# Splitting weight chunks in pairs instead of one by one, in a one-layer transformer kernel

## The reference

```python
x = layer_norm(a * x + 0.5 * swiglu(x, ffn1_gate, ffn1_up, ffn1_down), ...)   # d_ff 5504
x = layer_norm(a * x + hybrid_mixer(x, w_in, cmp_..., w_out), ...)            # stick-breaking and sparse attention
x = layer_norm(a * x + memory_cross_attention(x, mem, mem_wq, mem_wk, mem_wv, mem_wo), ...)
x = layer_norm(a * x + 0.5 * swiglu(x, ffn2_gate, ffn2_up, ffn2_down), ...)
```

## Time and profile before

| what | value |
| --- | --- |
| median of 3 runs | 2330.62 us (2328.92 to 2330.88) |
| profiled execution, span from first to last instruction | 2327.1 us |
| median of the runs less that span | 3.5 us |
| mean granted TensorE clock | 0.990 |
| TensorE matmul busy | 2263.6 us (97%) |
| VectorE busy | 1218.7 us (52%) |
| ScalarE busy | 1019.0 us (44%) |

### The profile page before, as it was taken

How to read it: one execution, slowest core, us unless ns; L and a number is a source line. 1 busy time by engine, 2 the same in 40 slices (tenths; PEclk the granted TensorE clock), 3 DMA queues, 4 the chain that set the end, 5 groups by cost and what they waited for, 6 DMA issues and landing times.

```text
span 2327.1 us, 26221 instructions
## 1 busy us (share of the span) xinstructions
PE 2263.6 (97%) x10486; PEld 1883.4 (81%) x10486; DVE 1218.7 (52%) x1269; ACT 1019.0 (44%) x1088; POOL 48.1 (2%) x34
## 2 busy tenths in 40 slices
PE   8999999999999999999999999997999999999996
PEld 6888888888888788888888877786888888898885
DVE  4544544455446545467556664456544454454445
ACT  4444444344334455555454443334444444443332
POOL 0000000000001100000000020001000000000001
PEclk9999999999999999999999999998999999999998
DMA  7555555465555455557346544453555555575552
GB/s 254 188 191 184 195 181 197 163 239 190 193 193 212 156 184 175 177 168 272 120 134 218 180 163 145 152 192 126 189 189 185 193 182 196 169 241 193 192 192 80
DMA packets 217084, 427.17 MB, mean 184 GB/s; under 512 B 6832, under 2 KB 23472, under 8 KB 216368
## 3 DMA queue, kind: packets, MB, share of 16 engines
q1 hardware_dynamic: 214336, 413.16, 52.5%
q10 hardware_dynamic: 2672, 12.93, 1.5%
HBM read 423.97 MB, written 2.10 MB: 183 GB/s over the span
## 4 chain that ended last, share of the span: by engine, by line
PE 93%; DVE 4%; ACT 1%; DMA 1%; issue 1%; POOL 0%; ACTq 0%; DVEq 0%; POOLq 0%
PE ps_A L489 45%; PE ps_B L489 42%; PE ps_T L505 2%; DVE wlo L921 2%; DVE x_tok L1359 1%; PE ps_T L864 1%; PE ps_T L851 1%; ACT whi L911 0%; PE ps_B L767 0%; PE ps_T L793 0%; DVE x_tok L1364 0%; DMA raw<-in_mem_wk_dram 0%; DMA stage<-in_mem_dram 0%; PE ps_T L638 0%; PE ps_T L802 0%
## 5 line engine op out<-in xcount | busy, mean ns | idle before, releaser
L921 DVE TENSOR_TENSOR wlo<-raw,whi 128x1024 fp32r<-128x1024 f32 (+1 forms) x792 | 965.9, 1222 | 1048.4 <-ACT whi L911 1047.4
L911 ACT ACTIVATE whi<-raw 128x1024 fp32r<-128x1024 f32 (+1 forms) x792 | 827.6, 1047 | 1196.9 <-PE ps_A L489 638.5
L489 PE MATMUL ps_A<-whi,xT_hi 128*128 128x512 f32 (+1 forms) x704 | 275.3, 391 | 8.4 <-DVE wlo L921 4.5
L489 PE MATMUL ps_A<-whi,xT_lo 128*128 128x512 f32 (+1 forms) x704 | 272.4, 387 | 0.0
L489 PE MATMUL ps_A<-wlo,xT_hi 128*128 128x512 f32 (+1 forms) x704 | 272.2, 387 | 0.0
L489 PE MATMUL ps_B<-whi,xT_hi 128*128 128x512 f32 (+1 forms) x704 | 270.3, 384 | 0.0
L489 PE MATMUL ps_B<-wlo,xT_hi 128*128 128x512 f32 (+1 forms) x704 | 270.3, 384 | 0.0
L489 PE MATMUL ps_B<-whi,xT_lo 128*128 128x512 f32 (+1 forms) x704 | 270.3, 384 | 0.0
L489 PEld LDWEIGHTS ps_A<-whi,xT_hi 128*128 128x128 f32 x704 | 133.3, 189 | 35.5 <-issue 8.8
L489 PEld LDWEIGHTS ps_A<-whi,xT_lo 128*128 128x128 f32 x704 | 133.1, 189 | 25.5
L489 PEld LDWEIGHTS ps_A<-wlo,xT_hi 128*128 128x128 f32 x704 | 133.4, 189 | 24.4
(11 more groups left out here) (279 smaller groups left out, 2864.2 us busy)
## 6 DMA issues: line engine op xcount, KB each, us to landing
raw<-in_ffn_gate_dram SPq DMA_DIRECT2D x80, 1024.0 KB, 4.9
raw<-in_ffn_up_dram SPq DMA_DIRECT2D x80, 1024.0 KB, 4.8
raw<-in_ffn_down_dram SPq DMA_DIRECT2D x80, 1024.0 KB, 5.1
raw<-in_w_in_dram SPq DMA_DIRECT2D x44, 1024.0 KB, 4.9
raw<-in_mem_wk_dram SPq DMA_DIRECT2D x16, 1024.0 KB, 5.1
raw<-in_mem_wv_dram SPq DMA_DIRECT2D x16, 1024.0 KB, 5.1
raw<-in_w_out_dram SPq DMA_DIRECT2D x16, 1024.0 KB, 5.1
raw<-in_mem_wq_dram SPq DMA_DIRECT2D x16, 1024.0 KB, 5.1
```

Of the source, the lines that this page charges most:

```text
L489: mm = pe.matmul(ps[pair][:, t * W:t * W + n], lhs[a][:, kt, t * P:(t + 1) * P], w[:, slot, q * n:(q + 1) * n], start=first and q == 0 and ...
L911: act.activation(whi[:, c % AHEAD, 0:n], raw[:, slot, o:o + n], ACT.Copy).then_inc(hi_made, 1)
L921: dve.tensor_tensor(wlo[:, c % AHEAD, 0:n], raw[:, slot, o:o + n], whi[:, c % AHEAD, 0:n].bitcast(F32), ALU.subtract).then_inc(lo_made, 1)
```

## The change

One ScalarE instruction and one VectorE instruction now split two neighbouring chunks, 128x2048 elements, where the chunks are full. The ring of four places is used as two places of two chunks. `make_hi` and `make_lo` do nothing for even c; for odd c they treat chunks c-1 and c together. `make_hi` waits until both chunks that held the place are multiplied, and the semaphores go up by 2. TensorE's code, the DMAs and the number of bytes in SBUF are the same.

```diff
+        def pair_of(c):
+
+            slot, s0, n, last = c // 2 % NRAW, (c - 1) % AHEAD, size(c - 1), size(c)
+            if last == n:
+                return [raw[:, slot, 0:2 * n].rearrange("p (s w) -> p s w", s=2), whi[:, s0:s0 + 2, 0:n],
+                        wlo[:, s0:s0 + 2, 0:n]]
+            return [raw[:, slot, 0:n + last]] + [w[:, s0:s0 + 2, :].rearrange("p s w -> p (s w)")[:, 0:n + last]
+                                                 for w in (whi, wlo)]
+
         def make_hi(act, c, i=None):
 
-            if c >= C_END:
+            if c >= C_END or c % 2 == 0:
                 return
-            slot, n = c // 2 % NRAW, size(c)
-            o = c % 2 * (CHUNK if n == CHUNK // 2 else n)
-            if c % 2 == 0:
-                act.wait_ge(landed[slot], plus(i, 32, 16 * (c // 8 + 1)))
+            w, hi, lo = pair_of(c)
+            act.wait_ge(landed[c // 2 % NRAW], plus(i, 32, 16 * (c // 8 + 1)))
             if c >= AHEAD:
                 act.wait_ge(multiplied, plus(i, 16, c - AHEAD + 1))
-            act.activation(whi[:, c % AHEAD, 0:n], raw[:, slot, o:o + n], ACT.Copy).then_inc(
-                hi_made, 1)
+            act.activation(hi, w, ACT.Copy).then_inc(hi_made, 2)
 
         def make_lo(dve, c, i=None):
 
-            if c >= C_END:
+            if c >= C_END or c % 2 == 0:
                 return
-            slot, n = c // 2 % NRAW, size(c)
-            o = c % 2 * (CHUNK if n == CHUNK // 2 else n)
+            w, hi, lo = pair_of(c)
             dve.wait_ge(hi_made, plus(i, 16, c + 1))
-            dve.tensor_tensor(wlo[:, c % AHEAD, 0:n], raw[:, slot, o:o + n],
-                              whi[:, c % AHEAD, 0:n].bitcast(F32), ALU.subtract).then_inc(
-                lo_made, 1)
+            dve.tensor_tensor(lo, w, hi.bitcast(F32), ALU.subtract).then_inc(lo_made, 2)
```

## The result

The changed kernel takes 2352.16 us (median of 4 runs, 2349.84 to 2354.4), the kernel before 2329.77 us on the same chips: ratio 1.0098, 95% interval 1.0083 to 1.0112. That is 22.4 us slower; forecast was 15.6 us, 2346.2 us, with a range of 2337 to 2360. Every run on record lies 1.7 to 1.9 us above its own span, so the profiled execution of the kernel before (2328.92 us) was one of the two faster of its four runs (2328.7, 2328.92, 2330.62 and 2330.88 us); of the 3.5 us that the forecast added to the span, 1.8 belong to that execution and 1.7 are the scatter of the runs. The mean granted clock of the changed kernel's profile is 0.985 (0.990 before).

The account below looks back on a forecast made before the run. TensorE, busy 97% of the span, was taken as the bound, with its waits for splits deciding. Terms 3.8 + 3.6 + 1.2 + 0.3 + 6.2 + 0.5 = 15.6 us on 2327.1, plus 3.5 for the runs: 2346.2 us, range 2337 to 2360.

Parts of the forecast that it names:

- the clock falls in CMP: Rival, 8%: TensorE idles 1.2 us in each 3.3 in CMP and drops to 1.2 GHz; +7 us, 2353.
- Saved engine time is worth nothing: Over some 396 pairs ScalarE gets 80 us back and VectorE 60, all inside idle time: 0 on the path.
- Plain blocks keep 0.86 us of slack: In plain blocks a pair's latency of 4.58 us stays under TensorE's 5.44 us of cover, costing 0.
- The rival that these blocks stall: Rival, 8%: latency over 5.44 us makes each of about 350 plain pairs pay the excess; about 2400 us.
- Matmul spacing by instruction traffic: Rival, 5%, faster: splits' instruction traffic spaces the matmuls, so halving their number shortens each chunk; 2314 at 0.04 us a chunk.
- Start, 3.6: At the kernel's start chunk 0 waits for chunk 1 too, and chunk 2's low part ends later again; 3.6 us.
- Short pairs, 3.8: Stalls of 0.42 us before each of two down products and 0.50 at six down-block ends; 3.8 us.
- Norms 1 and 2, 0.6 each: First two norms: later first chunk of w_in, less a slow-clock chunk hidden in K0; net 0.6 us each.
- The schedule's +2.9: At a norm, first chunk of w_in comes at 32.1 us from the down product's end instead of 29.2.
- Third norm, 0.3: One split between the third norm's pieces grows from 1.21 to 2.30 us, mostly taken back; 0.3 us (0 to 1.1).
- CMP, 6.2: In CMP the two-place loop takes 6.5 us, a pair every 3.3, and the second pair enters late; +6.2 us.
- Rest, 0.5: w_in, FILL and memory attention: only about 0.5 us (0 to 2), in V2 and at the first wq block's end.

Follow-up runs that it names:

- e3: Changed kernel with single chunks at the start, the down blocks' beginnings and in CMP, pairs elsewhere: 2330.34 us, ratio 1.0005 to the kernel before.
- e7: Changed kernel with the pair's ScalarE copy in the plain blocks of FFN 1 cut into 4 instructions of 512 elements: 2348.02 us, one run.
- e8: Changed kernel with the pair's ScalarE copy in the plain blocks of FFN 1 cut into 16 instructions of 128 elements: 2375.54 us, one run.
- e2: Changed kernel with single chunks at the start (chunks 0 to 3) and for the first two chunks of each down block: 2339.62 us, ratio 1.0039.
- e6: Changed kernel with ScalarE still copying pairs, but VectorE subtracting the two chunks one after the other and signalling each: 2338.01 us, ratio 1.0035.
- e4: Changed kernel with single chunks everywhere except the pairs behind norm_add in the first two norms: 2327.6 us, ratio 0.9993 to the kernel before.
- e9: Changed kernel with single chunks everywhere except the pairs around all three layer norms: 2328.2 us, ratio 0.9998 to the kernel before.
- e5: Changed kernel with eight thrown-away TensorE transposes ahead of every CMP pair but the first: 2346.11 us, ratio 1.0073.

## Why the prediction was right, and where it was off

The direction, the mechanism of the ring and the places were right; the sum was 8 us short in the profiled execution (23.6 against 15.6), 6.8 us in the medians. The measured 2352.2 us lie nearer to the rival "the clock falls in CMP" (8%, priced at 2353) than to the forecast's 2346.2, and the changed kernel's profile is that rival's case on top of the forecast chain. Point by point, in the order of the forecast:

- **Saved engine time is worth nothing.** Right. 135 us of busy time went into waits, and e3 shows that the pairs outside the three places neither cost nor bring anything beyond its interval. The rule of the Trainium skill on fixed latency ("VectorE: DVE Perf Modes", section on the TRN2 errata) names a saving of engine time that the rows have; the path does not have it.
- **Plain blocks keep 0.86 us of slack.** Right in what it says of the time: 21.76 us after. The slack is 0.72 by the rows, and e7 and e8 bracket it between 0.28 and 1.39. The rival that these blocks stall is refuted. Its price was wrong as well: each plain pair would have paid half the excess, not all of it (e8).
- **Matmul spacing by instruction traffic.** Refuted: half the splits, and in e7 four times the copies, with the same 21.76.
- **Start, 3.6.** Measured 3.9, which is in part luck: the delay of chunk 2 was 3.1, and 1.3 us of low clock stood behind it, less 0.5 that came back. e2 takes all of it away, and 1.1 more.
- **Short pairs, 3.8.** The eight places are the right ones; a ninth stall, ahead of K0, is there too and hidden behind the norm. Each cost 0.64 to 0.78 us instead of 0.42 to 0.50, together 5.9. Two things were missed: handovers of 0.28 and 0.10 us, which I had read as 0.20 and 0.03 in one place of the trace, and the wider spacing of the first matmuls behind a wait. My upper bound of 6.4 held.
- **Norms 1 and 2, 0.6 each.** Measured 0.0 and 0.1. The move of the slow clock into K0 is there and gave 2.2 us back (forecast 2.3). The schedule's +2.9 was +2.1: from the copy behind the down product to w_in's first matmul, 743.08 to 774.37, are 31.3 us, where 29.2 stood before. The bound that I had put on the low side, GpSimd's cost once for each instruction, is what e6 and the rows show, though its -4 us was never near: e4 gained 1.7 and 2.3 us at the two norms, e9 1.4 and 2.8.
- **Third norm, 0.3.** Measured -0.5, below its bound of 0; no experiment explains the sign, and e9 shows no gain there.
- **CMP, 6.2.** The loop is right: 6.3 in e2 and 6.35 in e5, both at a clock of 1.00. That the total agrees to a tenth is luck, since a turn took 6.6 to 6.8 us instead of 6.5 and the second pair was late by 2.8 us at the entry instead of 2. And I forecast it as the whole cost and gave the clock's fall 8%; the profiled execution paid 4.7 us for it on top (I had priced it at 7). This step is where the forecast was wrong: "no row shows a fall after an idle this short". The absence of a row in a kernel that never idled so was no evidence, and the idle is longer than the 1.2 us that I had put there, 1.9 to 2.6 us ahead of every second pair. The rule that I set beside the rival (the Trainium skill, "TensorE: Matmul & The Clock Gate", "HAM oscillation": idle gaps that recur between short groups of matmuls bring the clock down) agrees with the changed kernel's trace, 0.57 to 0.72 in CMP, and not with e2's, 1.00 with the same waits. That section's own example has longer waits than these, for DMAs, so my sentence that by this rule the 7 us would be paid went further than it does. In e5, with the gaps filled, the clock stayed up.
- **Rest, 0.5.** 0.6 in the memory attention and w_in, and 2.5 in FILL from a clock that falls there in kernels with single chunks too (e4, e9) and in nine of the eleven profiles. No term of mine allowed for it, and it may not be the change's.

Slow clock in CMP (4.7), FILL (2.5) and short pairs (2.1 over) make 9.3 us; the norms give back 1.9; start and the rest add 0.4. That is the 8 us, within rounding.

What stays open: why the same waits in CMP come with a lowered clock in one execution and not in another, what brings it down in FILL, and whether the kernel before has that fall in most of its runs too.

## What to carry to other kernels

Where the bound engine consumes from a ring, ask for the latency from "place free" to "place ready" and for the work that lies beside it, not for the producers' busy share: fusing two items made the first 4.7 us instead of 2.65 here and halved the number of places, and every stretch whose work is shorter than the latency then stalls. With two places a stage runs at (latency + own work) / 2, so an excess costs half in a steady stretch and in full at a single short item. Fuse only where the producer itself is on the path (the norms here; e4 and e9 gain 1.4 to 2.8 us at each of the first two in their profiles, which their runs do not tell from no change), and release fused work in parts if the consumer can start on one. Where the producer is on the path, weigh that against what the parts cost: e6 lost 2.75 us at the first norm by it.

## What was not expected of the hardware

- A VectorE subtraction beside GpSimd's work on x_tok pays about the same for 2048 elements (3.32 to 3.38 us against 2.29, +1.0 to +1.1) as for 1024 (2.04 in the earlier trace rows and 2.31 in the row below against 1.22, +0.8 to +1.1). From VectorE's timeline before:

```profile
750.49 2.31 DVE L921 TENSOR_TENSOR wlo<-raw,whi 128x1024 fp32r<-128x1024 f32 x1
```

- After a wait of 0.50 us the first two matmuls start 0.31 us apart instead of 0.227, at a granted clock that shows no fall.
- The granted clock fell in FILL to a mean of 0.59 over 8 us with TensorE busy for all of them (e4), and stayed at 1.00 in CMP with waits of 2.3 to 2.6 us in every 6.7 (e2).
